# Norm of the query latent: its four tiles' squares are added on VectorE, and TensorE sums one tile instead of four

## The chip, the cores and the metric

The kernel runs on one core of one Trainium2 chip. The metric is the device time of one execution, in microseconds (us). Lower is better.

## The reference, cut to what matters

The program is two blocks one after the other: a gated convolution and attention block with its feed-forward part, then a block with an RWKV7 mixer and a latent attention mixer (MLA), each with residual and norms. The change lies at the start of the latent attention mixer:

```
def _rms_norm(x, g):
    xf = x.astype(jnp.float32)
    y = xf * lax.rsqrt(jnp.mean(xf * xf, axis=-1, keepdims=True) + RMS_EPS)
    return (y * g.astype(jnp.float32)).astype(x.dtype)

def _mla_mixer(x, pos, w_in, q_norm, w_q_up, kv_norm, w_kv_up, w_out):
    B, L, _ = x.shape
    H = MLA_HEADS                                   # 16
    h = x @ w_in
    c_q, c_kv, k_rope, g = jnp.split(h, [Q_LORA, Q_LORA + KV_LORA, Q_LORA + KV_LORA + QK_ROPE], axis=-1)
    q = (_rms_norm(c_q, q_norm) @ w_q_up).reshape(B, L, H, QK_NOPE + QK_ROPE)
    q_nope, q_rope = q[..., :QK_NOPE], _rope(q[..., QK_NOPE:], pos)
    kv = (_rms_norm(c_kv, kv_norm) @ w_kv_up).reshape(B, L, H, QK_NOPE + V_HEAD)
    k_nope, v = kv[..., :QK_NOPE], kv[..., QK_NOPE:]
    k_rope = _rope(k_rope, pos)
    o = _causal_block_attention(q_nope, q_rope, k_nope, k_rope, v).reshape(B, L, D_INNER)
    return (o * jax.nn.silu(g)) @ w_out
```

The query latent c_q has 512 features (4 tiles of 128), the key/value latent c_kv has 256 (2 tiles). There are 512 tokens, and 16 meta tokens ahead of them for the keys. The change is in how the mean of the squares of c_q is formed.

## The kernel before, in words

Features lie on the 128 partitions and tokens in the columns, so a norm's sum over features is a sum over partitions and tiles. ScalarE squares each tile into one of two slots of the buffer norm_sq (line 210). TensorE multiplies each slot with a 128 x 128 matrix of ones and accumulates all tiles in one PSUM bank (pe_tile, line 227). These operands are fp32, and the profile shows each such matmul as two. ScalarE then takes Ln (line 219) and Exp (line 221) for the reciprocal root.

Every matmul of the projections is three fp32r matmuls, high x high, low x high, high x low (product, lines 162 to 164). So each operand is split into a high and a low part. GpSimd splits the weights, unit by unit, with two instructions: w_hi (line 150) and w_lo (line 153). The split of unit u waits until TensorE has finished unit u - 2, whose buffer it takes. VectorE does the activations: for each latent tile a scaled product norm_y (line 245), a cast to the high part (line 250) and a subtraction for the low part (line 253).

The stretch around the change runs so. There are seven input units, 0 to 6, each of eight blocks of 128 features: units 0 to 3 make the query latent's tiles, 4 and 5 those of the key/value latent, 6 the rotary key. On TensorE come units 2, 3 and 4, the sums of norm_q, units 5 and 6, the sums of norm_kv, and then six "fills", products that prepare the first head: gate 0, rope, ka, qn, kb, gate 1 (lines 2822 to 2829 and the function fill at line 2312). Rope and qn need the query latent's four high and low parts, ka and kb those of the key/value latent. Kb also needs its bank back from the rope fill, which VectorE's first rope instruction (line 2424) reads. After the fills head 0 starts, and its first value product needs the weight unit "B 0", whose split on GpSimd waits for the end of VectorE's rope group (q_step, lines 2439 and 2441). GpSimd's splits are in the order: input units, gate 0, A 0 (weights of rope, ka, qn and kb), gate 1, B 0.

VectorE works through one fixed list (lines 2925 to 2972): the four tiles cq out of PSUM (line 2927), tile 0 of ckv (line 2933), cos_r and sin_r (lines 2937 and 2938), norm_q tiles 0 and 1, ckv tile 1 (line 2933), norm_q tiles 2 and 3, five small memsets (lines 2949 and 2950), the rotary key's product (line 2953), norm_kv tiles 0 and 1, the gate out of PSUM (line 2402), and the rope group (lines 2960 to 2968 and 2424 to 2441). ScalarE's list there is: the four squares of cq, Ln and Exp, the two squares of ckv, Ln and Exp, k_sw, the gate's Silu (line 2396), and the rope copies q_sw (line 2376, four instructions) that the rope instruction of line 2424 waits for. Since the Silu is ahead of q_sw and waits for line 2402, the rope group follows line 2402.

The counters: sq_ready counts squares done, sq_summed tiles summed. The square of tile j waits for sq_summed to show that its slot has been read.

Of the kernel before, what the change touches and what calls it, by code (L numbers as in the profile page):

```python
# [12 lines left out]
ALU = mybir.AluOpType  # L13
# [57 lines left out]
def program(nc, io, out):  # L71
    with ExitStack() as base:
        def sb(name, shape, dt=F32, stack=base):
            return stack.enter_context(nc.sbuf_tensor(name, shape, dt))
# [4 lines left out]
        def sem(name):  # L79
            return base.enter_context(nc.semaphore(name))  # L80
# [19 lines left out]
        ps = base.enter_context(nc.psum_tensor("ps", [P, 8, 512], F32))  # L100
# [3 lines left out]
        ones = sb("ones", [P, P])  # L104
# [21 lines left out]
        def prm(name, j=0, n=1):  # L126
            return params[:, COL[name] + j:COL[name] + j + n]
# [5 lines left out]
        def load_unit(sp, u, s, src, first=False):  # L133
            if not first:
                sp.wait_ge(split_ready, u - 1)
            _, k, n = src.shape
            sp.dma_start(raw[s][:, 0:k * n].rearrange("p (k n) -> p k n", k=k), src).then_inc(landed[s], 16)
# [36 lines left out]
        sq_ready = sem("sq_ready")  # L174
        sq_summed = sem("sq_summed")
# [10 lines left out]
        class Norm:  # L186
# [12 lines left out]
                tiles_before[0] += tiles  # L199
                norms_before[0] += 1  # L200

            def act(self, act, wait_x, last=None):
                for j in range(self.tiles):
                    wait_x(act, j)
                    if self.t0 + j >= 2:
                        act.wait_ge(sq_summed, self.t0 + j - 1)
                    dst, src = self.sq[:, j % 2, 0:self.cols], self.x(j)
                    if last is not None and j == self.tiles - 1:
                        dst, src = dst.rearrange("p (a b) -> p a b", a=2), last
                    nc.scalar.activation(dst, src, ACT.Square).then_inc(sq_ready, 1)  # L210
                self.act_r(act)
# [12 lines left out]
            def pe_tile(self, pe, j):  # L224
                pe.wait_ge(sq_ready, self.t0 + j + 1)
                for h, (at, n) in enumerate(self.halves):
                    mm = nc.tensor.matmul(ps[:, self.bank + h, 0:n], ones[:], self.sq[:, j % 2, at:at + n],  # L227
                                          start=(j == 0), stop=(j == self.tiles - 1))
                mm.then_inc(sq_summed, 1)

            def pe(self, pe):
# [39 lines left out]
            def act_parts(self, act, hi, p0):  # L271
                for j in range(self.tiles):
                    act.wait_ge(y_ready, self.t0 + j + 1)
                    nc.scalar.activation(hi(j), self.y[:, j % 4, 0:self.cols], ACT.Copy).then_inc(act_hi_ready, 1)
# [1881 lines left out]
        norm_q = Norm(lambda j: cq[:, j, :], 4, HALVES1, 512, lambda j: prm("qn", j), 6, put.end)  # L2156
# [15 lines left out]
        s_tab, in_ev, k_step = sem("s_tab"), sem("in_ev"), sem("k_step")  # L2172
# [525 lines left out]
        with nc.Block() as block:  # L2698
# [75 lines left out]
            def _(pe):  # L2774
# [11 lines left out]
                def in_unit(n, banks, parts):  # L2786
                    u = U_IN + n
                    pe.wait_ge(split_ready, u + 1)
                    for k in range(KD):
                        for b, (at, cols) in zip(banks, parts):  # L2790
                            mm = product(ps[:, b, 0:cols], block_of(slot_of(u), k), (u2_hi[:, k, at:at + cols], u2_lo[:, k, at:at + cols]),
                                         k == 0, k == KD - 1)
                    mm.then_inc(unit_done, 1)
# [10 lines left out]
                for i, j in enumerate(WO_ORDER):  # L2804
# [3 lines left out]
                    for t in range(QB):  # L2808
                        mm = nc.tensor.transpose(ps[:, 2 + i % 2, P * t:P * t + P], xT[:, j, N_META + P * t:N_META + P * t + P], ident[:])
# [9 lines left out]
                in_unit(2, (2,), TAIL)  # L2819
                in_unit(3, (3,), TAIL)  # L2820
                in_unit(4, (4, 5), HALVES2)
                norm_q.pe(pe)
                pe.wait_ge(in_ev, 2)
                in_unit(5, (0, 1), HALVES2)
                pe.wait_ge(in_ev, 4)
# [9 lines left out]
            def _(act):  # L2835
# [5 lines left out]
                               last=ps[:, WO_BANKS[WO_ORDER[-1]][0]:WO_BANKS[WO_ORDER[-1]][1] + 1, 0:T2 // 2])  # L2841

                def rows_out(i):
                    j = WO_ORDER[i]
                    act.wait_ge(x_turned, KD + i + 1)
                    nc.scalar.activation(h_rows[:, :, P * j:P * j + P], ps[:, 2 + i % 2, :].rearrange("p (a b) -> p a b", b=P),
                                         ACT.Copy).then_inc(x_copied, 1)
# [6 lines left out]
                        rows_out(i - 1)  # L2854
                norm_pre1.act_r(act)
                rows_out(KD - 1)
                norm_q.act(act, lambda e, j: e.wait_ge(in_ev, j + 1))
                norm_kv.act(act, lambda e, j: e.wait_ge(in_ev, j + 5))
                act.wait_ge(k_step, 3)
                for q in range(4):  # L2860
# [14 lines left out]
                for half in range(2):  # L2875
                    act.wait_ge(o_mm, QB + half)
                    at = (t, 2 * QB)[half]
# [10 lines left out]
            def _(dve):  # L2888
                front_dve(dve)
                all_passes(dve, pass_dve)  # L2890
                for j, m in enumerate(WO_ORDER):
                    dst = mT[:, m, :].rearrange("p (a b) -> p a b", a=2)
# [32 lines left out]
                for m in range(4):  # L2925
                    dve.wait_ge(unit_done, U_IN + m + 1)
                    nc.vector.tensor_tensor(cq[:, m, :], ps[:, m, :], r_pre1[:, N_META:T2], ALU.mult).then_inc(in_ev, 1)
                two = lambda ap: ap.rearrange("p (a b) -> p a b", a=2)

                def ckv_out(m):  # L2930
# [93 lines left out]
```

## Time and profile before

| what | value |
|---|---|
| time, median of 3 runs | 2260.21 us (2258.67 to 2261.58) |
| the profiled execution's own time | 2259.74 us |
| its span | 2258.0 us |
| granted TensorE clock in the span | 0.998 of full speed |
| busy: TensorE | 2226.6 us, 99% |
| busy: VectorE | 1212.6 us, 54% |
| busy: ScalarE | 838.4 us, 37% |
| busy: GpSimd | 1155.2 us, 51% |
| matmuls in the span | 21811 |

The span is the time from the first to the last instruction in the trace; the execution's own time is 1.74 us longer. PE is TensorE, DVE VectorE, ACT ScalarE, POOL GpSimd. A row of the timeline gives start and length of an instruction in us, then in brackets how long the engine had stood idle before it and what released it. A busy TensorE may still be waiting in part: the ends of its matmuls are modelled, so a stall shows best in its weight loads.

### The profile page before, as it was taken

Reading aid. Unit: us, or ns where it says so; the run is one execution under the profiler, and the core shown is the slowest. Engines: PE = TensorE matmul, PEld = TensorE weight load, DVE = VectorE, ACT = ScalarE, POOL = GpSimd, SP = SyncE. Lnnn points to the kernel's source line nnn. Section 1 sums busy time; section 2 is a strip of 40 time slices with the busy share of each in tenths; the row PEclk is TensorE's granted clock in tenths of the full one; section 3 lists DMA queues with packets and bytes.
Section 4 is the critical chain, followed back from the end, with each engine's and each line's share of the span. In section 5 each row is a group of like instructions: output and inputs, shape, how many; then the busy total and the mean of one; then the engine's idle time right before and its main releaser. Section 6 shows DMA issues by size and latency. Waiting matters only on the chain.

```text
span 2258.0 us, 51404 instructions
## 1 busy us (share of the span) xinstructions
PE 2226.6 (99%) x21811; PEld 1798.7 (80%) x21811; DVE 1212.6 (54%) x2314; ACT 838.4 (37%) x1725; POOL 1155.2 (51%) x802
## 2 busy tenths in 40 slices
PE   8999999999999999999999999999999999999998
PEld 7788888788888677777777777777889788888877
DVE  4353357877830955555555555666540475555521
ACT  4122212333310455555555555555421344434311
POOL 4555567687766163444444444444636353443454
PEclk9999999999999999999999999999999999999999
DMA  3323333333332122222222222222413322212132
GB/s 117 85 76 83 80 88 93 94 94 99 97 105 92 49 90 67 70 77 72 73 79 84 72 70 71 77 70 97 167 55 112 113 71 56 64 51 55 52 126 89
DMA packets 262108, 188.04 MB, mean 83 GB/s; under 512 B 18283, under 2 KB 242409, under 8 KB 261497
## 3 DMA queue, kind: packets, MB, share of 16 engines
q1 hardware_dynamic: 261881, 184.76, 27.3%
q8 instruction: 174, 2.85, 0.5%
q14 instruction: 53, 0.43, 0.1%
HBM read 162.69 MB, written 22.04 MB: 82 GB/s over the span
## 4 chain that ended last, share of the span: by engine, by line
PE 94%; DVE 3%; POOL 1%; ACT 1%; SPq 0%; issue 0%; DMA 0%; DVEq 0%; POOLq 0%; ACTq 0%
PE ps L1359 20%; PE ps L162 17%; PE ps L163 16%; PE ps L164 16%; PE ps L1545 3%; PE ps L1561 3%; PE ps L1587 2%; PE ps L2509 2%; PE ps L1534 2%; PE ps L1372 1%; PE ps L1501 1%; PE ps L227 1%; PE ps L1473 1%; PE ps L1490 1%; PE ps L1523 1%; PE ps L1459 1%
## 5 line engine op out<-in xcount | busy, mean ns | idle before, releaser
L153 POOL TENSOR_TENSOR w_lo<-raw,w_hi 128x1024 fp32r<-128x1024 f32 (+1 forms) x164 | 418.8, 2554 | 13.7
L150 POOL TENSOR_SCALAR w_hi<-raw 128x1024 fp32r<-128x1024 f32 (+1 forms) x164 | 181.6, 1107 | 450.5 <-PE ps L164 434.5
L162 PE MATMUL ps<-h_hi,w_hi 128*128 128x512 f32 x616 | 243.8, 396 | 1.8 <-DVE h_lo L1068 1.7
L164 PE MATMUL ps<-h_hi,w_lo 128*128 128x512 f32 x616 | 240.6, 391 | 0.0
L163 PE MATMUL ps<-h_lo,w_hi 128*128 128x512 f32 x616 | 240.3, 390 | 0.0
L1359 PE MATMUL ps<-mixed_k,raw 128*64 128x264 f32 x1024 | 149.3, 387 | 0.0
L1359 PE MATMUL ps<-mixed_r,raw 128*64 128x264 f32 x1024 | 143.9, 387 | 0.0
L1359 PE MATMUL ps<-mixed_g,raw 128*64 128x264 f32 x1024 | 138.0, 386 | 0.0
L162 PEld LDWEIGHTS ps<-h_hi,w_hi 128*128 128x128 f32 x616 | 116.2, 189 | 25.9 <-DVE h_lo L1068 2.5
L164 PEld LDWEIGHTS ps<-h_hi,w_lo 128*128 128x128 f32 x616 | 116.0, 188 | 24.9
L163 PEld LDWEIGHTS ps<-h_lo,w_hi 128*128 128x128 f32 x616 | 116.2, 189 | 23.1
L1359 PE MATMUL ps<-mixed_v,raw 128*64 128x264 f32 x1024 | 129.0, 389 | 0.0
L1083 DVE SCALAR_TENSOR_TENSOR up_c<-up_raw,params,up_c 128x512 f32<-128x512 f32 x88 | 114.5, 1304 | 22.7 <-ACT up_c L838 21.1
L1887 DVE TENSOR_TENSOR x_m<-ps,lv_pad 128x640 f32<-128x640 f32 (+2 forms) x160 | 110.9, 726 | 9.7 <-PE ps L1545 5.2
L1951 POOL TENSOR_TENSOR kp<-k_b,kp 128x528 f32<-128x528 f32 x16 | 29.6, 1850 | 168.8 <-ACT kp L1680 168.8
L1545 PEld LDWEIGHTS ps<-t_m,mb 128*64 128x64 f32 x2752 | 95.9, 138 | 15.6 <-ACT mb L1668 3.4
L1545 PE MATMUL ps<-t_m,mb 128*64 128x64 f32 x2752 | 97.3, 222 | 0.2 <-DVE t_m L1893 0.2
L1359 PEld LDWEIGHTS ps<-mixed_v,raw 128*64 128x64 f32 x1024 | 69.6, 137 | 34.2 <-issue 2.5
L1968 POOL MEMSET uv<- 64x64 f32 x32 | 4.6, 145 | 175.2 <-PE ps L1516 174.3
L2615 ACT ACTIVATE xT<-ps,nmax 128x144 f32<-128x144 f32 (+1 forms) x64 | 34.4, 539 | 147.3 <-DVE nmax L2642 146.9
L1634 ACT ACTIVATE uv<-ps 64x64 f32<-64x64 f32 x128 | 27.9, 218 | 161.6 <-PE ps L1490 161.6
L1561 PEld LDWEIGHTS ps<-x_m,t_t 128*64 128x64 f32 x2240 | 77.5, 138 | 9.6 <-DVE x_m L1887 0.6
(473 smaller groups left out, 5973.4 us busy)
## 6 DMA issues: line engine op xcount, KB each, us to landing
raw<-in_rwkv_w_in_dram SPq DMA_DIRECT2D x64, 512.0 KB, 4.2
raw<-in_w_up_dram SPq DMA_DIRECT2D x44, 512.0 KB, 3.8
raw<-in_w_in_dram SPq DMA_DIRECT2D x41, 512.0 KB, 3.9
raw<-in_w_down_dram SPq DMA_DIRECT2D x22, 512.0 KB, 3.6
raw<-in_mla_w_in_dram SPq DMA_DIRECT2D x22, 512.0 KB, 4.1
sb_kept<-xT SPq DMA_DIRECT2D x16, 528.0 KB, 2.7
xT<-sb_kept SPq DMA_DIRECT2D x16, 528.0 KB, 4.6
raw<-in_rwkv_w_out_dram SPq DMA_DIRECT2D x16, 512.0 KB, 3.9
```

Of the source, the lines that this page charges most:

```text
L150: nc.gpsimd.tensor_scalar(w_hi[s][:, 0:width], raw[s][:, 0:width], 1.0, 0.0, ALU.mult, ALU.add).then_inc(split_hi, 1)
L153: nc.gpsimd.tensor_tensor(w_lo[s][:, 0:width], raw[s][:, 0:width], w_hi[s][:, 0:width].bitcast(F32), ALU.subtract).then_inc(split_ready, 1)
L162: nc.tensor.matmul(dst, w[0], x[0], start=start, stop=False)
L163: nc.tensor.matmul(dst, w[0], x[1], start=False, stop=False)
L164: return nc.tensor.matmul(dst, w[1], x[0], start=False, stop=stop)
L1083: nc.vector.scalar_tensor_tensor(out=up_c[:, ab, 1 + k, :], in0=up_raw[:, n % 4, 1 - k:1 - k + T1], scalar=prm(("cf1", "cf0")[k], n // 2 + ...
L1359: mm = nc.tensor.matmul(dst[m, :], raw_k[t % 2][:, k, m], mixed[t][:, k, cols], start=(k == 0), stop=(k == KD - 1))
L1534: mm = nc.tensor.matmul(ps[:, 2 + 3 * h + q, x * P:x * P + P], bk[own[h], c0 + x, :], rkv[own[h], c0 + x, 0:2 * C], start=True, stop=True)
L1545: mm = nc.tensor.matmul(ps[own[h], 2 + p, x * C:x * C + C], mb[:, c0 + x, own[h]], t_m[:, c0 + x, :], start=True, stop=True)
L1561: mm = nc.tensor.matmul(dst, t_t[:, c0 + x, :], x_m[:, c0 + x, h, :], start=True, stop=True)
L1587: mm = nc.tensor.matmul(ps[m, 6 + h, 0:T2 // 2], halves_ones[:, m], src(h), start=True, stop=True)
L1887: nc.vector.tensor_tensor(x_m[:, c0:c0 + m, :, :], part_of(2 + p, m).unsqueeze(2).to_broadcast([P, m, 2, C]), lv_pad[:, lv - 1, :, :].unsq ...
```

## The change

In norm_q alone, ScalarE still squares four tiles, but tile 0 goes to slot 0 and tiles 1, 2 and 3 all go to slot 1. After each of tiles 1 to 3 VectorE adds slot 1 to slot 0. TensorE then multiplies slot 0 once with the ones. The adds and the one sum count up sq_summed as the four sums did.

```diff
-            def act(self, act, wait_x, last=None):
+            def act(self, act, wait_x, last=None, added=False):
                 for j in range(self.tiles):
                     wait_x(act, j)
                     if self.t0 + j >= 2:
                         act.wait_ge(sq_summed, self.t0 + j - 1)
-                    dst, src = self.sq[:, j % 2, 0:self.cols], self.x(j)
+                    dst, src = self.sq[:, min(j, 1) if added else j % 2, 0:self.cols], self.x(j)
...
+            def dve_add(self, dve, j):
+                dve.wait_ge(sq_ready, self.t0 + j + 1)
+                if j >= 2:
+                    dve.wait_ge(sq_summed, self.t0 + j - 1)
+                acc = self.sq[:, 0, 0:self.cols]
+                nc.vector.tensor_tensor(acc, acc, self.sq[:, 1, 0:self.cols], ALU.add).then_inc(sq_summed, 1)
+
+            def pe_slot(self, pe, slot, first, last):
+                for h, (at, n) in enumerate(self.halves):
+                    mm = nc.tensor.matmul(ps[:, self.bank + h, 0:n], ones[:], self.sq[:, slot, at:at + n], start=first, stop=last)
                 mm.then_inc(sq_summed, 1)
...
                 in_unit(4, (4, 5), HALVES2)
-                norm_q.pe(pe)
+                pe.wait_ge(sq_summed, norm_q.t0 + norm_q.tiles - 1)
+                norm_q.pe_slot(pe, 0, True, True)
                 pe.wait_ge(in_ev, 2)
...
-                norm_q.act(act, lambda e, j: e.wait_ge(in_ev, j + 1))
+                norm_q.act(act, lambda e, j: e.wait_ge(in_ev, j + 1), added=True)
...
                 for m in range(4):
                     dve.wait_ge(unit_done, U_IN + m + 1)
                     nc.vector.tensor_tensor(cq[:, m, :], ps[:, m, :], r_pre1[:, N_META:T2], ALU.mult).then_inc(in_ev, 1)
+                    if m:
+                        norm_q.dve_add(dve, m)
```

On VectorE, from the query latent's first tile on, the list before is (cq, ckv: the latents' tiles; ps: PSUM; r_pre: the factor of the norm ahead of the mixer):

```order
L2927 TENSOR_TENSOR cq<-ps,r_pre 128x512 [waits unit_done,rs_ready]
L2927 TENSOR_TENSOR cq<-ps,r_pre 128x512 [waits unit_done] x3
L2933 TENSOR_TENSOR ckv<-ps,r_pre 128x528 [waits unit_done]
L2937 TENSOR_TENSOR cos_r<-cos_t,r_pre 128x528 [waits s_tab,in_ev]
L2938 TENSOR_TENSOR sin_r<-sin_t,r_pre 128x528
L245 SCALAR_TENSOR_TENSOR norm_y<-cq,params,norm_r 128x512 [waits rs_ready]
```

and with the change:

```order
L2940 TENSOR_TENSOR cq<-ps,r_pre 128x512 [waits unit_done,rs_ready]
L2940 TENSOR_TENSOR cq<-ps,r_pre 128x512 [waits unit_done]
L236 TENSOR_TENSOR norm_sq<-norm_sq 128x512 [waits sq_ready]
L2940 TENSOR_TENSOR cq<-ps,r_pre 128x512 [waits unit_done]
L236 TENSOR_TENSOR norm_sq<-norm_sq 128x512 [waits sq_summed,sq_ready]
L2940 TENSOR_TENSOR cq<-ps,r_pre 128x512 [waits unit_done]
L236 TENSOR_TENSOR norm_sq<-norm_sq 128x512 [waits sq_summed,sq_ready]
L2948 TENSOR_TENSOR ckv<-ps,r_pre 128x528 [waits unit_done]
L2952 TENSOR_TENSOR cos_r<-cos_t,r_pre 128x528 [waits s_tab,in_ev]
L2953 TENSOR_TENSOR sin_r<-sin_t,r_pre 128x528
L257 SCALAR_TENSOR_TENSOR norm_y<-cq,params,norm_r 128x512 [waits rs_ready]
```

Each of the last three tiles of cq has an add behind it that waits for that tile's square. Everything from ckv on keeps its order; lines 245, 250, 253, 2927 and 2933 are lines 257, 262, 265, 2940 and 2948 of the changed kernel.

On TensorE, from the last product of input unit 4 to the first of unit 5, the list before is:

```order
L162 MATMUL ps<-u_hi,w_hi 128x264
L163 MATMUL ps<-u_lo,w_hi 128x264
L164 MATMUL ps<-u_hi,w_lo 128x264
L227 MATMUL ps<-norm_sq,ones 128x512 [waits sq_ready] x4
L162 MATMUL ps<-u_hi,w_hi 128x264 [waits split_ready,in_ev]
L163 MATMUL ps<-u_lo,w_hi 128x264
```

and with the change:

```order
L162 MATMUL ps<-u_hi,w_hi 128x264
L163 MATMUL ps<-u_lo,w_hi 128x264
L164 MATMUL ps<-u_hi,w_lo 128x264
L240 MATMUL ps<-norm_sq,ones 128x512 [waits sq_summed]
L162 MATMUL ps<-u_hi,w_hi 128x264 [waits split_ready,in_ev]
L163 MATMUL ps<-u_lo,w_hi 128x264
```

Three of four sums are gone, and the one left waits for the adds (sq_summed) in place of the squares (sq_ready).

## Rows read from the trace of the kernel before

**Rows 1.** First line of the page.

```profile
span 2258.0 us, 51404 instructions
```

**Rows 2.** Busy us (and instructions) by engine in one stretch, PEclk, DMA share, GB/s.

```profile
1860.00:2030.00 170.00, 170.00 (x1015) 144.78 (x1014) 90.42 (x240) 70.36 (x140) 72.58 (x41) 1.00 0.21 57
```

**Rows 3.** Chain that ended last, in order: start us, us, what.

```profile
1804.08 3.62 PE ps L227 x8
...
1837.01 1.27 POOL w_hi L150
...
1841.36 0.39 PE ps L162
```

**Rows 4.** Timeline of TensorE's weight loads: start, length, instruction, [idle before <-releaser].

```profile
1804.34 0.19 PEld L227 LDWEIGHTS ps<-norm_sq,ones 128*128 128x128 f32 x1 [0.24 <-issue]
1804.77 0.19 PEld L227 LDWEIGHTS ps<-norm_sq,ones 128*128 128x128 f32 x1 [0.24 <-issue]
...
1805.71 0.30 PEld L227 LDWEIGHTS ps<-norm_sq,ones 128*128 128x128 f32 x2 [0.75 <-ACT norm_sq L210]
```

**Rows 5.** Timeline of ScalarE around the norm of the query latent.

```profile
1805.03 0.63 ACT L210 ACTIVATE norm_sq<-cq 128x512 f32<-128x512 f32 x1 [16.78 <-PE ps L227]
```

**Rows 6.** Timeline of VectorE, from the latent's last tile to the first gate.

```profile
1798.31 0.69 DVE L2927 TENSOR_TENSOR cq<-ps,r_pre 128x512 f32<-128x512 f32 x1 [4.87 <-PE ps L164]
...
1805.91 2.87 DVE L2938 TENSOR_TENSOR sin_r<-sin_t,r_pre 128x528 f32<-128x528 f32 x1
...
1809.12 0.75 DVE L245 SCALAR_TENSOR_TENSOR norm_y<-cq,params,norm_r 128x512 f32<-128x512 f32 x1 [0.35 <-ACT norm_r L221]
...
1813.53 0.71 DVE L2933 TENSOR_TENSOR ckv<-ps,r_pre 128x528 f32<-128x528 f32 x1 [0.62 <-PE ps L164]
...
1815.40 2.51 DVE L250 CAST cq_hi<-norm_y 128x512 fp32r<-128x512 f32 x1
...
1819.80 1.62 DVE L253 TENSOR_TENSOR cq_lo<-norm_y,cq_hi 128x512 fp32r<-128x512 f32 x1
...
1822.59 2.20 DVE L245 SCALAR_TENSOR_TENSOR norm_y<-ckv,params,norm_r 128x528 f32<-128x528 f32 x1 [0.25 <-ACT norm_r L221]
...
1827.19 1.43 DVE L253 TENSOR_TENSOR ckv_lo<-norm_y,ckv_hi 128x528 fp32r<-128x528 f32 x1
...
1828.54 0.68 DVE L2402 TENSOR_TENSOR gate<-ps,r_pre 128x512 f32<-128x512 f32 x1
```

**Rows 7.** Timeline of GpSimd: the splits of the weight units in this stretch.

```profile
1799.69 2.40 POOL L153 TENSOR_TENSOR w_lo<-raw,w_hi 128x1024 fp32r<-128x1024 f32 x1
...
1805.51 2.70 POOL L153 TENSOR_TENSOR w_lo<-raw,w_hi 128x1024 fp32r<-128x1024 f32 x1
...
1813.78 1.05 POOL L150 TENSOR_SCALAR w_hi<-raw 128x1024 fp32r<-128x1024 f32 x1 [5.57 <-PE ps L164]
...
1814.92 2.71 POOL L153 TENSOR_TENSOR w_lo<-raw,w_hi 128x1024 fp32r<-128x1024 f32 x1
...
1819.61 1.27 POOL L150 TENSOR_SCALAR w_hi<-raw 128x1280 fp32r<-128x1280 f32 x1 [1.98 <-PE ps L164]
...
1820.96 3.27 POOL L153 TENSOR_TENSOR w_lo<-raw,w_hi 128x1280 fp32r<-128x1280 f32 x1
...
1826.92 1.14 POOL L150 TENSOR_SCALAR w_hi<-raw 128x1024 fp32r<-128x1024 f32 x1 [2.69 <-PE ps L164]
```

**Rows 8.** Instructions of four VectorE lines: ns min/median/max, first and last start us, forms.

```profile
L245 DVE SCALAR_TENSOR_TENSOR norm_y<-cq,params,norm_r x4: 746/750/1211, 1809.1 to 1818.6; 128x512 f32<-128x512 f32 x4
...
L250 DVE CAST cq_hi<-norm_y x4: 426/428/2506, 1809.9 to 1819.3; 128x512 fp32r<-128x512 f32 x4
...
L253 DVE TENSOR_TENSOR cq_lo<-norm_y,cq_hi x4: 693/693/1619, 1810.4 to 1819.8; 128x512 fp32r<-128x512 f32 x4
...
L1059 DVE TENSOR_TENSOR ffn_sq<-ffn_sq x6: 687/1232/1376, 351.1 to 378.3; 128x512 f32<-128x512 f32 x6
```

**Rows 9.** Timeline of TensorE: first matmul of the fill ka.

```profile
1829.21 0.28 PE L162 MATMUL ps<-ckv_hi,w_hi 128*128 128x264 f32 x1
```

More of the change, by code:

```diff
@@ L228, in pe_tile @@
                                           start=(j == 0), stop=(j == self.tiles - 1))
+                mm.then_inc(sq_summed, 1)
+            def dve_add(self, dve, j):
[7 more added lines that the diff above has]
+                    mm = nc.tensor.matmul(ps[:, self.bank + h, 0:n], ones[:], self.sq[:, slot, at:at + n], start=first, stop=last)
                 mm.then_inc(sq_summed, 1)
```

## The prediction

> **What bounds the kernel now.** I read the page first, then the chain of waits and the timelines of all four engines from 1798 to 1842 us, where the changed instructions lie. The span is 2258.0 us [rows 1], and the execution that was profiled took 2259.74 us. TensorE is the bound nearly everywhere: between 1860 and 2030 us it was busy for the whole 170.00 us at full clock, with VectorE at 90.42 and GpSimd at 72.58 us [rows 2]. A microsecond that TensorE gains or loses before 1860 us therefore reaches the end. But the chain doesn't stay on TensorE in the stretch itself. From the sums of the key/value norm it runs over ScalarE and VectorE to GpSimd's split of unit B 0 at 1837.01 us and comes back to TensorE only at 1841.36 us [rows 3]. So two clocks run side by side from 1804 to 1841 us, TensorE's and VectorE's, and the later one decides.
>
> **What the change removes on TensorE.** The four sums take 3.62 us of the chain [rows 3]. Each is two passes of 512 columns. The weight loads of successive passes start at 1804.34 and 1804.77, so a pass costs 0.43 us and a sum 0.86 us; 4 x 0.86 = 3.44 us, and the rest is a wait for squares that ScalarE could only make once sum 0 had freed its slot: it stood idle for 16.78 us before the third square [rows 5], and the weight load for it began at 1805.71 after 0.75 us of idleness [rows 4]. One sum of 0.86 us is left, so TensorE starts unit 5 about 3.62 - 0.86 = 2.76 us earlier. Bounds: 3 x 0.86 = 2.58 us if the wait was hidden in part, 2.9 us at most.
>
> **What it adds on VectorE.** Three adds of two SBUF tiles, 128 x 512 fp32. The same operation stands elsewhere in this program at line 1059, with 0.687 us at least and 1.376 us at most [rows 8]; alone it is 0.69 us. Only the last could delay the sum. Tile 3 of cq starts at 1798.31 and takes 0.69 us [rows 6], its square 0.63 us [rows 5], so the add can start at 1799.7 us, just when GpSimd begins a w_lo of 2.40 us [rows 7]. If it has to wait for that, it ends near 1802.7 us; TensorE asks at 1803.9 us (0.17 us before the chain's 1804.08), and ckv tile 0, the next item of VectorE's list, is not released before 1804.1. If the add goes first, GpSimd ends its split near 1802.7 us in place of 1802.09, and TensorE needs it at 1804.8 us. The adds cost nothing at either end; the covers are 1.2 and 2.1 us. For the earlier adds VectorE has some 5 us of idle time each, as in the 4.87 us ahead of 1798.31. ScalarE no longer waits for sum 0, and Ln and Exp of norm_q end at about 1806.3 us.
>
> **What is late next.** The question is what VectorE makes of the 2.76 us. sin_r keeps it busy to 1808.78 us in any case (1805.91 + 2.87), which is only 0.35 us before it took up norm_q tile 0 in the trace [rows 6]. The other idle times on its path to the last low part of ckv are 0.62 us ahead of ckv tile 1 and 0.25 us ahead of norm_kv: 1.22 us in all. So VectorE can't gain more than 1.2 us, while TensorE comes 2.8 us earlier.
>
> It can lose, though, by GpSimd. Rows 8 give the three steps of a tile at 0.75, 0.43 and 0.69 us when undisturbed, but 1.21, 2.51 and 1.62 us at most. Each long one stands beside a split: the cast that started at 1815.40 ended at 1817.91, 0.28 us after GpSimd's w_lo (1814.92 + 2.71 = 1817.63); the low part from 1819.80 waited for the w_hi of 1819.61, norm_y from 1822.59 for the w_lo of 1820.96, the low part from 1827.19 for the w_hi of 1826.92, and sin_r for the w_lo of 1805.51 [rows 6, 7]. Instructions that read PSUM (ckv at 1813.53, the gate at 1828.54) were not lengthened. GpSimd is held back as well: its w_lo take 2.70, 2.71 and 3.27 us where one without VectorE beside it takes 2.40. So one of the two runs at a time. A waiting VectorE instruction ends 0.15 us less than its length after GpSimd's end, and GpSimd's waiting instruction 0.14 us less than its length after VectorE's end: 2.26 us for w_lo (1817.63 against 1815.37, just ahead of the cast), 2.81 us for the wide one of A 0 (1824.23 against 1821.42).
>
> In the trace these stalls on VectorE's path are 0.46 + 2.08 (gate 0), 0.93 + 1.44 (A 0) and 0.72 us (gate 1) = 5.6 us. The splits are released by TensorE, so they all come 2.76 us earlier, at 1811.02, 1816.85 and 1824.16 us, and VectorE's list comes only 0.35 us earlier. I walk through it with these lengths (ends of instructions, us):
> - norm_y 0 starts at 1808.72; norm_y 1 ends at 1811.33. w_hi of gate 0 was waiting, ends 1812.24; cast 1 1812.52; w_lo 1814.78; low part 1 1815.32; ckv tile 1 1815.96; its square 1816.6, still in time for TensorE's second sum of norm_kv at about 1817.2.
> - norm_y 2 1816.64; cast 2 1817.11; w_hi of A 0 1818.24; low part 2 1818.78; w_lo 1821.59; norm_y 3 1822.19; cast 3 1822.66; low part 3 1823.38. The memsets and the key product take 0.9 us as before (1821.42 to 1822.59 less 0.25 of idleness).
> - norm_kv: norm_y 0 would start at 1824.25, w_hi of gate 1 is ahead of it at 1824.16 and ends 1825.21; norm_y 0 1825.82; w_lo 1828.08; cast 0 1828.37; low part 0 1829.12; norm_y 1 1829.80; cast 1 1830.27; low part 1 1831.01.
>
> The stalls are now 0.7 + 2.1, 0.95 + 2.7 and 0.8 + 2.1 = 9.4 us, 3.7 more, against 1.2 us less idle time. What was hidden under TensorE's sums was that the splits fell beside waits and PSUM reads: the w_lo of gate 1 met the gate's PSUM read at 1828.54 and now meets the cast. Before, the low part ended at 1828.62 (1827.19 + 1.43), 0.6 us before TensorE began ka at 1829.21 [rows 9]. Now TensorE asks at 1829.21 - 2.76 = 1826.45 us and waits some 4.6 us. The end is 1831.01 - 1828.62 = 2.4 us later than before.
>
> That is handed on. Behind the low part come the gate (1830.9), the Silu, four q_sw and the rope group, which releases B 0's split and also kb's bank. Each followed the one before it directly in the trace, so the split of 1837.01 and TensorE's return at 1841.36 [rows 3] come 2.4 us later, and TensorE's own work between ka and there, some 12 us, starts 1.9 us late and gets its other 0.5 us as a wait for kb's bank. **Sum: 2.4 us slower.** Against the profiled execution 2259.74 + 2.4 = 2262.1 us; the median of the three runs stands 0.47 us above that execution, which gives 2260.21 + 2.4 = 2262.6 us. I take the second.
>
> **A rule of the Trainium skill beside this.** The row is sin_r: 2.87 us at 1805.91, against 0.69 us for a subtraction of two SBUF tiles by itself [rows 6, 8]. The Trainium skill, page "SBUF — State Buffer", section "Who interferes with whom", says that a VectorE instruction with two SBUF inputs, or in a two-port mode, and a GpSimd instruction that reads SBUF lock each other out, that the earlier one has the shared pair for its whole length, and that a VectorE instruction with at most one SBUF input and outside those modes goes free. By that rule the trace agrees, and the rule decides an order that I can't know: if norm_y 0 of norm_kv takes the lock ahead of w_hi at 1824.2 us, the same walk ends at 1830.9 us in place of 1831.0. If the two shared in proportion and nobody waited for a whole instruction, the stalls would stay near 5.6 us and the first rival below would hold.
>
> **The rivals.**
> - A, the stalls stay as they are (5.6 us), because the order in which waiting instructions get through isn't the one of my walk. VectorE's path then ends 1.2 us earlier, at 1827.4 us, later than TensorE's 1826.45, so VectorE sets the time: 2260.2 - 1.2 = 2259.0 us. For it: I have only five stalls to read the order from. Against: all five fit.
> - B, TensorE's gain goes through whole: 2260.2 - 2.8 = 2257.4 us. For it: TensorE is the 99% engine. Against: VectorE would have to reach the last low part of ckv by 1826.4 us, 2.2 us before its old end, with only 1.2 us of idle time to give; a split would have to miss it altogether.
> - C, slower by over 0.2%: a further w_lo falls on VectorE's path, in the rope group or in head 0. Its place would be B 0's or gate 2's split against the instructions that TensorE's first attention products wait for. Its price is one more stall of up to 2.7 us, the largest of the walk, so 2.4 + 2.7 = 5.1 us and 2265.3 us. It decides if the shift isn't the same on GpSimd and VectorE after 1837 us. Against: B 0's split is released by VectorE's own group, so both shift together.
>
> **How the numbers follow.** The forecast has a chance of 0.64, A 0.14, B 0.10, C 0.12. What a measurement of this kernel can tell from no change is about 0.2%, 4.5 us. The forecast lies inside it unless the spread of the runs (2258.67 to 2261.58) adds 2 us (0.04), A and B lie inside, C lies just over it (0.07 of its 0.12). So: slower 0.11, faster 0.03, within 0.2% 0.86. The range runs from 2257.8 us (A and part of B's spread) to 2265.2 us (most of C). The forecast by itself spans 2261.1 to 2264.1 us, the same width as the three runs.
>
> **What would show each step.** Right: one sum with two passes ends near 1804.8 us; the adds end before 1803.9; unit 5 starts 2.8 us earlier; a cast or low part beside each w_lo is 2.5 to 2.8 us long; norm_y 3 is near 3.5 us; the last low part of ckv ends near 1831 us; TensorE's weight loads show a gap of 4 to 5 us ahead of ka; B 0's split starts near 1839.4 us. Wrong: ka follows rope with no gap (B), or a gap near 1 us and B 0's split at 1835.8 (A), or an add or a late split ahead of the sum or of unit 5, which would upset the 2.76 us itself.

## The result, and the profile after

The changed kernel takes 2263.21 us (median of 20 runs, 2260.99 to 2266.79) against 2260.45 us (20 runs, 2258.63 to 2261.93) for the kernel before. The ratio is 1.0014 with a 95% interval of 1.0008 to 1.002: it is slower, by 2.8 us, less than the 0.2% that the forecast called no change. The forecast was 2262.6 us, with a range of 2257.8 to 2265.2 us.

The page of the changed kernel, first line and the line of busy times (engine, us, share of the span, instructions):

```profile
span 2260.9 us, 51397 instructions
...
PE 2225.9 (98%) x21805; PEld 1801.3 (80%) x21805; DVE 1223.5 (54%) x2317; ACT 840.9 (37%) x1725; POOL 1157.2 (51%) x802
```

VectorE has three instructions more and TensorE six fewer, as the change says; the span is 2.9 us longer [rows 1]. Of these 2.9 us, 0.69 us were there before the stretch in question: ckv tile 0 starts at 1804.80 us against 1804.11. Executions of one kernel differ by as much and more ahead of 1800 us (e5 and e12 below are one kernel and start this tile at 1802.51 and 1804.37 us), so from here on times are taken from the start of ckv tile 0, in what I call the **interval**: from there to head 0's first value product (w_hi, ckv_hi) on TensorE. Before it is 1841.36 - 1804.11 = 37.25 us.

VectorE's timeline of the changed kernel, with the lines that answer to [rows 6]:

```profile
1799.01 0.69 DVE L2940 TENSOR_TENSOR cq<-ps,r_pre 128x512 f32<-128x512 f32 x1 [3.48 <-PE ps L164]
1800.40 2.93 DVE L236 TENSOR_TENSOR norm_sq<-norm_sq 128x512 f32<-128x512 f32 x1 [0.70 <-ACT norm_sq L210]
1804.80 0.71 DVE L2948 TENSOR_TENSOR ckv<-ps,r_pre 128x528 f32<-128x528 f32 x1 [1.47 <-PE ps L164]
...
1806.60 2.90 DVE L2953 TENSOR_TENSOR sin_r<-sin_t,r_pre 128x528 f32<-128x528 f32 x1
1809.42 0.74 DVE L257 SCALAR_TENSOR_TENSOR norm_y<-cq,params,norm_r 128x512 f32<-128x512 f32 x1
...
1812.05 1.15 DVE L262 CAST cq_hi<-norm_y 128x512 fp32r<-128x512 f32 x1
1813.24 2.77 DVE L265 TENSOR_TENSOR cq_lo<-norm_y,cq_hi 128x512 fp32r<-128x512 f32 x1
1815.93 0.69 DVE L2948 TENSOR_TENSOR ckv<-ps,r_pre 128x528 f32<-128x528 f32 x1
...
1817.78 1.62 DVE L265 TENSOR_TENSOR cq_lo<-norm_y,cq_hi 128x512 fp32r<-128x512 f32 x1
1819.32 3.45 DVE L257 SCALAR_TENSOR_TENSOR norm_y<-cq,params,norm_r 128x512 f32<-128x512 f32 x1
...
1824.80 0.76 DVE L257 SCALAR_TENSOR_TENSOR norm_y<-ckv,params,norm_r 128x528 f32<-128x528 f32 x1
1825.60 1.16 DVE L262 CAST ckv_hi<-norm_y 128x528 fp32r<-128x528 f32 x1
1826.79 2.73 DVE L265 TENSOR_TENSOR ckv_lo<-norm_y,ckv_hi 128x528 fp32r<-128x528 f32 x1
...
1830.71 0.71 DVE L265 TENSOR_TENSOR ckv_lo<-norm_y,ckv_hi 128x528 fp32r<-128x528 f32 x1
1831.34 0.69 DVE L2414 TENSOR_TENSOR gate<-ps,r_pre 128x512 f32<-128x512 f32 x1
```

And GpSimd's, which answer to [rows 7]:

```profile
1800.39 2.40 POOL L153 TENSOR_TENSOR w_lo<-raw,w_hi 128x1024 fp32r<-128x1024 f32 x1
...
1811.72 1.20 POOL L150 TENSOR_SCALAR w_hi<-raw 128x1024 fp32r<-128x1024 f32 x1 [2.79 <-PE ps L164]
1813.01 2.45 POOL L153 TENSOR_TENSOR w_lo<-raw,w_hi 128x1024 fp32r<-128x1024 f32 x1
1817.55 1.32 POOL L150 TENSOR_SCALAR w_hi<-raw 128x1280 fp32r<-128x1280 f32 x1 [2.09 <-PE ps L164]
1818.94 3.28 POOL L153 TENSOR_TENSOR w_lo<-raw,w_hi 128x1280 fp32r<-128x1280 f32 x1
1824.86 1.61 POOL L150 TENSOR_SCALAR w_hi<-raw 128x1024 fp32r<-128x1024 f32 x1 [2.64 <-PE ps L164]
1826.56 2.41 POOL L153 TENSOR_TENSOR w_lo<-raw,w_hi 128x1024 fp32r<-128x1024 f32 x1
1839.81 1.26 POOL L150 TENSOR_SCALAR w_hi<-raw 128x1280 fp32r<-128x1280 f32 x1 [10.85 <-DVE qr L2453]
```

The last add waited for the w_lo of 1800.39 and took 2.93 us, and was done 1.5 us before ckv tile 0. sin_r kept its 2.90 us. Then come the stalls: cast 1 took 1.15 us and low part 1 2.77 us beside gate 0's split (1811.72 and 1813.01), low part 2 1.62 us and norm_y 3 3.45 us beside A 0's (1817.55 and 1818.94), and in norm_kv cast 0 1.16 us and low part 0 2.73 us beside gate 1's (1824.86 and 1826.56). Each ends 0.3 to 0.6 us after a GpSimd instruction does. The last low part of ckv ends at 1831.42 us, 26.62 us after ckv tile 0 began; before it was 24.51 us.

TensorE's weight loads, and the first value product on TensorE (these answer to [rows 3, 4, 9]):

```profile
1804.49 0.31 PEld L240 LDWEIGHTS ps<-norm_sq,ones 128*128 128x128 f32 x2
1805.04 0.19 PEld L162 LDWEIGHTS ps<-u_hi,w_hi 128*128 128x128 f32 x1 [0.24 <-issue]
...
1831.54 0.19 PEld L162 LDWEIGHTS ps<-ckv_hi,w_hi 128*128 128x128 f32 x1 [4.65 <-issue]
```

```profile
1844.30 0.36 PE L162 MATMUL ps<-w_hi,ckv_hi 128*128 128x256 f32 x1
```

The one sum's two loads are at 1804.49 and unit 5's first at 1805.04. Ahead of ka TensorE stood for 4.65 us by its loads (4.26 by the matmuls' own idle time) and began it at 1831.57 us, which is 1.67 us later in the interval than in [rows 9]. The interval is 1844.30 - 1804.80 = 39.50 us, 2.25 us longer than before; with the 0.69 us from ahead of it this makes the 2.9 us of the span.

One thing the forecast had not: the clock. The stretches in and behind the gap (us, busy us of PE, PEld, DVE, ACT, POOL with counts, granted clock, DMA share, GB/s):

```profile
1827.00:1831.50 4.50, 0.31 (x2) 0.00 (x0) 4.43 (x5) 1.66 (x2) 1.96 (x1) 1.00 0.27 67
1831.50:1833.50 2.00, 1.93 (x8) 1.79 (x9) 1.85 (x3) 1.41 (x3) 0.00 (x0) 0.62 0.37 111
1833.50:1835.50 2.00, 2.00 (x6) 1.62 (x5) 0.36 (x1) 1.95 (x4) 0.00 (x0) 0.52 0.00 0
1835.50:1837.50 2.00, 2.00 (x13) 1.75 (x13) 1.97 (x5) 0.63 (x2) 0.00 (x0) 1.00 0.00 0
```

After 4.3 us of idleness the granted clock was 0.62 and then 0.52 in two windows of 2 us. Full speed is 2.4 GHz and the lower level 1.2 GHz, 0.5 of it, so TensorE stood at the lower level for 0.76 + 0.96 of a window, 3.4 of these 4.0 us. In the kernel before it was 1.00 throughout this stretch.

### The profile page after: what moved, and what is told of

Read it like the earlier page. It is cut to its first block, busy times and chain, and to the rows that moved or that the text cites. A ratio compares the mean times of both kernels' runs of the same rounds, so it can differ in the third digit from the quotient of the medians.

```text
span 2260.9 us, 51397 instructions
## 1 busy us (share of the span) xinstructions
PE 2225.9 (98%) x21805; PEld 1801.3 (80%) x21805; DVE 1223.5 (54%) x2317; ACT 840.9 (37%) x1725; POOL 1157.2 (51%) x802
## 4 chain that ended last, share of the span: by engine, by line
PE 94%; DVE 3%; POOL 1%; ACT 1%; SPq 0%; issue 0%; DMA 0%; DVEq 0%; POOLq 0%; ACTq 0%
PE ps L1371 20%; PE ps L162 17%; PE ps L163 16%; PE ps L164 16%; PE ps L1557 3%; PE ps L1573 3%; PE ps L1599 2%; PE ps L2521 2%; PE ps L1546 2%; PE ps L1384 1%; PE ps L1513 1%; PE ps L1485 1%; PE ps L1502 1%; PE ps L1535 1%; PE ps L1471 1%; PE ps L2504 1%
## 5 line engine op out<-in xcount | busy, mean ns | idle before, releaser
L162 PEld LDWEIGHTS ps<-h_hi,w_hi 128*128 128x128 f32 x616 | 115.8, 188 | 26.2 <-DVE h_lo L1080 2.8
L1095 DVE SCALAR_TENSOR_TENSOR up_c<-up_raw,params,up_c 128x512 f32<-128x512 f32 x88 | 119.1, 1357 | 20.3 <-ACT up_c L850 18.7
```

The lines of the kernel that those rows point to most:

```text
L162: nc.tensor.matmul(dst, w[0], x[0], start=start, stop=False)
L1095: nc.vector.scalar_tensor_tensor(out=up_c[:, ab, 1 + k, :], in0=up_raw[:, n % 4, 1 - k:1 - k + T1], scalar=prm(("cf1", "cf0")[k], n // 2 + ...
```

## The experiments

Each kernel was timed 11 times beside the kernel before on the same chip. A time comparison of that size has a 95% interval of about 0.09% (2 us) to either side, so the medians decide little and the intervals inside the profiled executions decide most. There is one profiled execution of each kernel. The interval of one kernel repeated where that could be seen: the kernel that was run twice under two names (e5 and e12) showed 35.88 us both times. From the first value product to the end every execution took the same 416.6 to 416.7 us, so two spans differ by the start of ckv tile 0 and by the interval.

| kernel | interval, us | last low part of ckv, us after ckv tile 0 | ratio of times to before (95%) |
|---|---|---|---|
| before | 37.25 | 24.51 | |
| changed | 39.50 | 26.62 | 1.0014 (1.0008 to 1.002) |
| e1, no adds | 39.52 | 26.62 | 1.0012 (1.0003 to 1.002) |
| e2, three sums more | 37.07 | 24.33 | 0.9993 (0.9984 to 1.0002) |
| e8, one sum more | 38.98 | 26.08 | 1.0009 (1.0 to 1.0018) |
| e3, gate 1's split held | 37.39 | 23.86 | 0.9997 (0.9988 to 1.0006) |
| e4, gap filled | 39.35 | 26.62 | 1.0011 (1.0002 to 1.002) |
| e7, tables early | 37.91 | 25.17 | 0.9999 (0.999 to 1.0008) |
| e5 and again e12, early and held | 35.88, 35.88 | 22.34, 22.35 | 0.9996 (0.9987 to 1.0004), 0.9995 (0.9986 to 1.0004) |
| e6, early and held, on before | 37.33 | 23.78 | 1.0004 (0.9995 to 1.0013) |
| e9, q_sw first | 40.61 | 26.61 | 1.001 (1.0001 to 1.0019) |
| e10, q_sw first and gap filled | 37.93 | 26.62 | 1.0004 (0.9996 to 1.0013) |
| e11, rope first | 35.87 | 22.35 | 1.0 (0.9991 to 1.0009) |

**e1: are the adds to blame?** In dve_add the sum is left out; waits and counts stay.

```diff
-                nc.vector.tensor_tensor(acc, acc, self.sq[:, 1, 0:self.cols], ALU.add).then_inc(sq_summed, 1)
+                dve.sem_inc(sq_summed, 1)
```

> The changed kernel with the three adds left out (VectorE keeps their waits and counts up the semaphore), so that the norm of the query latent is taken over tile 0 alone. TensorE's and GpSimd's timing is that of the changed kernel. Theory L (GpSimd's splits and VectorE's list lock each other out once the splits come 2.8 us earlier; the adds cost nothing): the loss stays, 2.8 us over before as in the changed kernel (within 0.7 us), the last low part of ckv about 26.6 us after ckv tile 0 starts, a gap of 4 to 5 us ahead of ka. Rival R1 (the three adds on VectorE cost the time): back to before or below, at or under +0.5 us.

The interval is 39.52 us and the last low part comes after 26.62 us, both as with the adds, to 0.02 us. The time is 3.55 us over before by medians, at the edge of what was allowed. The three adds cost nothing; R1 falls.

**e2: TensorE's timing put back.**

```diff
+                for _ in range(3):
+                    nc.tensor.matmul(ps[:, 6, 0:512], ones[:], norm_q.sq[:, 0, 0:512], start=True, stop=True)
                 norm_q.pe_slot(pe, 0, True, True)
```

> The changed kernel with three sums of the same slot put ahead of the one sum on TensorE, so that TensorE reaches unit 5 nearly when it did before (4 x 0.86 = 3.44 us of sums against 3.62 us), while the adds stay. Theory L: the time is that of before, between -0.5 and +0.7 us, the last low part of ckv about 24.5 us after ckv tile 0 starts, no gap ahead of ka, no low clock there. R1 (the adds cost it): still +2.8 us.

VectorE's timeline of this kernel:

```profile
1802.67 0.71 DVE L2950 TENSOR_TENSOR ckv<-ps,r_pre 128x528 f32<-128x528 f32 x1 [1.47 <-PE ps L164]
...
1813.78 2.51 DVE L262 CAST cq_hi<-norm_y 128x512 fp32r<-128x512 f32 x1
...
1825.57 1.43 DVE L265 TENSOR_TENSOR ckv_lo<-norm_y,ckv_hi 128x528 fp32r<-128x528 f32 x1
```

The cast is 2.51 us and the last low part 1.43 us, the very durations of [rows 6]. The interval is 37.07 us, 0.18 us under before, which is what 3.44 us of sums in place of 3.62 give. The time's median is 1.5 us under before, outside the half microsecond that was allowed, with an interval that holds no difference; I take it for the spread of the runs. With the adds in place and only TensorE's work put back, the loss is gone: it comes from TensorE's earlier start.

**e8: half the shift.** The same edit with one sum more in place of three.

> The changed kernel with one more sum on TensorE (two in place of one; TensorE reaches unit 5 1.9 us earlier than before, in place of 2.76). Theory L gives by the walk: the last low part of ckv 26.2 us after ckv tile 0 starts (before 24.5, changed 26.6), interval to the first value product 38.9 us, time 1.7 us over before. A loss in proportion to TensorE's gain would be 1.9/2.76 of 2.25 us, 1.55 us; a loss by the clock after the gap alone would be smaller than that.

The interval is 38.98 us (38.9 expected) and the last low part 26.08 us (26.2). The walk through the locks holds for a shift it wasn't made from. In proportion it would have been 38.8 us, so the interval alone can't tell the walk from that. The single lengths can: the longest instructions were the cast of cq tile 2 (2.51 us), the low part of cq tile 3 (3.33 us) and the cast of ckv tile 1 (2.47 us), other ones than in the changed kernel. The median is 3.5 us over before where 1.7 were expected; the ratio's interval (0 to 4 us) holds both.

**e3: one split taken out of VectorE's way.**

```diff
             def split_mla(pool, u):
+                if u == UNIT_AT["gate", 1]:
+                    pool.wait_ge(y_lo_ready, CKV_READY)
```

> The changed kernel with one wait more on GpSimd: the split of weight unit gate 1 waits for the last low part of ckv. Theory L: the stalls of that split (0.8 + 2.1 us in the walk) leave VectorE's path; the last low part ends about 2.8 us earlier than in the changed kernel, the gap ahead of ka shrinks from 4.3 us to 1.5 to 2 us, and the time is 2.5 to 3.5 us under the changed kernel, which is before -0.4 us within 0.7. Rival R2 (the place where VectorE and GpSimd meet doesn't matter, TensorE is late for another reason, as the lower clock after the gap): no more than 1 us under the changed kernel.

Its VectorE timeline, from ckv tile 0 on:

```profile
1806.72 0.71 DVE L2950 TENSOR_TENSOR ckv<-ps,r_pre 128x528 f32<-128x528 f32 x1 [1.47 <-PE ps L164]
...
1827.51 0.43 DVE L262 CAST ckv_hi<-norm_y 128x528 fp32r<-128x528 f32 x1
1827.97 0.71 DVE L265 TENSOR_TENSOR ckv_lo<-norm_y,ckv_hi 128x528 fp32r<-128x528 f32 x1
...
1829.87 0.71 DVE L265 TENSOR_TENSOR ckv_lo<-norm_y,ckv_hi 128x528 fp32r<-128x528 f32 x1
```

Cast 0 and low part 0 of ckv are back at 0.43 and 0.71 us, from 1.16 and 2.73. The last low part ends 2.76 us earlier in the interval than in the changed kernel, the gap ahead of ka is 1.5 us, and the interval is 2.11 us shorter, 0.14 us over before. The time is 0.25 us under before by medians, as expected; the interval gave up less than the last low part did, since the held split now meets the rotary key's product (1.27 us in place of 0.70) and its sum (2.79 us in place of 0.71), and q_rot kept kb waiting for 1.6 us. So without this one pair of stalls 2.1 of the 2.25 us are gone. That TensorE's clock stayed at 1.00 behind the shorter gap is part of this edit too; e4 separates the two and leaves the clock, which R2 names, 0.15 us; R2 falls.

**e4: the gap filled with sums, for the clock.**

```diff
                 for n in range(6):
+                    if n == 2:
+                        for _ in range(5):
+                            nc.tensor.matmul(ps[:, 1, 0:512], ones[:], norm_q.sq[:, 0, 0:512], start=True, stop=True)
                     fill(pe, n)
```

> The changed kernel with five more sums (ten passes, 4.3 us) into a spare PSUM bank ahead of ka on TensorE, which fill the gap where TensorE waits for VectorE. In the changed kernel the granted clock was 0.62 and 0.52 of full in the 4 us behind that gap. Theory C (beside L: the idle gap lowers the clock; in the profiled execution B 0's split hides it, in others it lasts longer and costs up to 4 us, which is the upper group of the 20 runs at 2264.6 to 2266.8): clock 1.00 behind ka, median 0.5 to 1.5 us under the changed kernel, no run over 2264.5. If the clock costs nothing: the same median and the same spread. If the sums themselves delay ka: 0.3 us over it.

The clock stayed at 1.00 and the interval is 39.35 us, 0.15 us under the changed kernel. The median is 0.7 us under the changed kernel's, which was not timed beside it. Theory C is wrong in its second half: the upper group of times stayed (up to 2266.17 us in 11 runs), and in this profiled execution ckv tile 0 started only at 1808.40 us. Such differences are made ahead of the stretch, and the traces show where most of them come from: the granted clock falls there in some executions and not in others, though all kernels do the same work up to 1780 us. The windows from 1650 to 1700 us of e4, and then of e3:

```profile
1650.00:1700.00 50.00, 48.29 (x592) 40.25 (x590) 17.35 (x51) 9.95 (x26) 18.29 (x12) 0.93 0.19 54
```

```profile
1650.00:1700.00 50.00, 48.28 (x612) 40.42 (x612) 17.89 (x52) 11.77 (x29) 18.32 (x12) 1.00 0.22 65
```

A VectorE copy at 1662.46 us in e4 stands at 1662.30 in e3; its third follower stands at 1675.34 against 1672.39 us, so the low clock cost 2.8 us there. A clock of 0.97 between 1600 and 1700 us have e1, e4, e10 and e11, one of 0.98 between 0 and 100 us the changed kernel, e1, e3, e4, e9 and e11. Those with both reached ckv tile 0 at 1808.40 to 1808.49 us, those with one at 1804.80 to 1807.05, and those with neither at 1802.51 to 1804.37 us; before, at 1804.11, had its 0.98 between 400 and 500 us. The single times go with it: of the changed kernel's 20 runs the five of 2266.26 to 2266.79 us have a clock of 0.994 or 0.995 over the whole execution, the four of 2260.99 to 2261.33 us have 0.997. Why the clock falls at these places in one execution and not in another stays open.

**e7, e5, e6: an earlier start of VectorE's list.** cos_r and sin_r are made in VectorE's idle time between the tiles of cq.

```diff
                 for m in range(4):
...
+                    if m == 1:
+                        dve.wait_ge(s_tab, 64)
+                        nc.vector.tensor_tensor(cos_r[:], cos_t[:], r_pre1[:], ALU.mult).then_inc(k_step, 1)
+                    if m == 2:
+                        nc.vector.tensor_tensor(sin_r[:], sin_t[:], r_pre1[:], ALU.mult).then_inc(k_step, 1)
...
                 ckv_out(0)
-                dve.wait_ge(in_ev, 5)
-                dve.wait_ge(s_tab, 64)
-                nc.vector.tensor_tensor(cos_r[:], cos_t[:], r_pre1[:], ALU.mult).then_inc(k_step, 1)
-                nc.vector.tensor_tensor(sin_r[:], sin_t[:], r_pre1[:], ALU.mult).then_inc(k_step, 1)
```

e7 has this edit on the changed kernel, e5 has it with e3's, and e6 has both edits on the kernel before.

> The changed kernel with cos_r and sin_r early and gate 1's split where it was. Theory L: the last low part of ckv ends 25.3 us after ckv tile 0 starts, the interval to the first value product is 38.0 us, time 0.8 us over before (0 to 1.6). If only the start of VectorE's list counted and not the locks: 2.4 us under the changed kernel, at 37.1 us.

> The changed kernel with cos_r made behind tile 1 and sin_r behind tile 2 of cq, in VectorE's idle time there, and with gate 1's split held until the last low part of ckv. Theory L, by the same walk of locks: norm_y 0 waits for ScalarE and the w_lo of unit 6 and ends 4.4 us after ckv tile 0 starts, and the last low part of ckv ends 22.4 us after it, 2.1 us earlier than in before, so TensorE's gain comes through but for 0.6 us. From ckv tile 0 to head 0's first value product: 35.2 us (before 37.25, changed 39.50). Time 2.1 us under before (1.4 to 2.8). Rival R3 (the early cos_r and sin_r collide with splits 3 and 4 and delay unit 5 or the squares, so that the gain is lost): no better than the kernel with gate 1's split held alone.

> The kernel before with the same two edits (early cos_r and sin_r, gate 1's split held) and without the change to the norm. Theory L: norm_y 0 waits here for the reciprocal root and not for sin_r, so the early tables give nothing, and the held split takes 0.7 us off VectorE's path, of which TensorE can use 0.6 (0.45 us wait ahead of kb, 0.18 ahead of the first value product). Interval from ckv tile 0 to the first value product 36.6 us, time 0.6 us under before. If instead the gain of the kernel with both came from these edits alone, it would be 2.1 us under before here too.

For e7 the walk gave 25.3 and 38.0 us; measured 25.17 and 37.91. For e5 it gave 22.4 and 35.2; measured 22.34 and 35.88. VectorE and the first value product in e5:

```profile
1802.51 0.71 DVE L2955 TENSOR_TENSOR ckv<-ps,r_pre 128x528 f32<-128x528 f32 x1 [1.47 <-PE ps L164]
1804.75 2.11 DVE L257 SCALAR_TENSOR_TENSOR norm_y<-cq,params,norm_r 128x512 f32<-128x512 f32 x1 [1.54 <-ACT norm_r L221]
...
1824.14 0.71 DVE L265 TENSOR_TENSOR ckv_lo<-norm_y,ckv_hi 128x528 fp32r<-128x528 f32 x1
...
1826.67 2.79 DVE L2980 TENSOR_TENSOR cos_r<-cos_r,k_sw 128x528 f32<-128x528 f32 x1
```

```profile
1838.39 0.39 PE L162 MATMUL ps<-w_hi,ckv_hi 128*128 128x256 f32 x1 [0.19 <-POOL w_lo L153]
```

The last low part is where it should be. What I had missed is behind it: the sum of the rotary key (cos_r, 1826.67) stood for 2.79 us behind gate 1's held w_lo, and the rope group behind that. The same happened in e6 (2.79 us too), whose interval of 37.33 us is not the 36.6 us expected, though its last low part came 0.7 us earlier. So the two edits alone bring nothing on the kernel before, and together with the change they end 1.37 us under before.

**e9 and e10: what the lower clock costs.** Both have ScalarE's q_sw ahead of the gate's Silu on the changed kernel, which frees B 0's split from the gate; e10 has e4's sums too.

```diff
+                fill_out(act, FILLS[1])
                 gate_silu(act, 0)
-                for n in range(1, 5):
+                for n in range(2, 5):
                     fill_out(act, FILLS[n])
```

> The changed kernel with ScalarE's four q_sw ahead of the gate's Silu, so that the rope group no longer waits for the gate behind the last low part: VectorE's rope instruction ends 2 us earlier and B 0's split no longer decides. What is left is TensorE itself: the gap ahead of ka and the lower clock behind it. Interval from ckv tile 0 to the first value product, by TensorE alone: theory T (the gap of 4.3 us and 3.7 us at half clock together make TensorE just as late as B 0's split): 39.3 to 39.5 us, no gain over the changed kernel's 39.50. If the low clock costs nothing and only B 0's split counted: 38.3 us.

> The kernel with q_sw first, and five more sums (4.3 us) in TensorE's gap ahead of ka, which keep its clock at 1.00. Theory T: both causes of the lateness are gone but the gap: interval 38.3 us (ka 1.7 us later than in before, less the 0.6 us that before waited for kb's bank and B 0), 1.0 to 1.2 us under the kernel without the sums, and that difference is what the low clock costs. If the clock costs nothing: no difference between the two kernels.

Windows of e9, and then of e10, behind the gap (columns as above; the clock is the third value from the end):

```profile
1832.00:1834.00 2.00, 0.20 (x1) 0.23 (x2) 1.93 (x4) 1.30 (x2) 0.00 (x0) 0.71 0.75 195
1834.00:1836.00 2.00, 2.00 (x8) 1.90 (x9) 1.97 (x4) 1.02 (x2) 0.00 (x0) 0.50 0.22 67
1836.00:1838.00 2.00, 2.00 (x6) 1.51 (x6) 1.97 (x5) 0.00 (x0) 0.00 (x0) 0.50 0.00 0
1838.00:1840.00 2.00, 2.00 (x7) 1.56 (x6) 1.93 (x4) 0.00 (x0) 0.00 (x0) 0.59 0.00 0
1840.00:1842.00 2.00, 2.00 (x13) 1.74 (x13) 1.05 (x3) 1.60 (x3) 0.74 (x1) 1.00 0.00 0
```

```profile
1832.00:1834.00 2.00, 2.00 (x11) 1.39 (x10) 1.97 (x4) 0.99 (x3) 0.00 (x0) 1.00 0.66 197
...
1838.00:1840.00 2.00, 2.00 (x10) 1.64 (x9) 1.77 (x4) 0.73 (x1) 1.04 (x1) 1.00 0.00 0
```

Two kernels that differ in the filling alone: 40.61 and 37.93 us, 2.68 us apart. In e9 the clock was at the lower level for 6.8 us in all (1.2 + 2.0 + 2.0 + 1.6 us by the windows), longer than the 3.4 us of the changed kernel's execution, and cost more than the 1.0 to 1.2 us expected; the interval was to be 39.3 to 39.5 us. Why the stretch at the lower level was longer is open. These are one execution of each kernel, and e9's own time, 2266.00 us, was its second longest of 11; by the medians the two kernels are 1.3 us apart, so 2.68 us may be more than the filling is usually worth. In e9 TensorE is the last: the first value product waited for nothing, and B 0's split was itself released by TensorE. e10 came to 37.93 us where 38.3 was expected.

**e11: rope ahead of the rotary key.** e5 with q_sw first and VectorE's rope instructions ahead of the rotary key's two.

> The kernel with the tables early and gate 1's split held, and beside it q_sw ahead of the gate's Silu on ScalarE and the rope instructions ahead of the rotary key's two on VectorE, so that the w_lo of gate 1 falls into VectorE's wait for q_sw. In the kernel without this the rotary key's sum stood 2.79 us behind that w_lo, and B 0's split started 31.5 us after ckv tile 0. Theory L: the wait ahead of kb (1.6 us) goes, B 0's split starts at about 31.2 us, interval to the first value product 35.5 us (35.88 without this), time 1.7 us under before. If another instruction takes the lost lock in its place: 35.9 us or more.

The 2.79 us stall is gone and kb no longer waits, but B 0's split starts 31.57 us after ckv tile 0, hardly later than e5's 31.54, since the rotary key's instructions now stand between the rope instructions and the last part of the rope group. The interval is 35.87 us, so the edit brings nothing; what had been a wait of 1.6 us ahead of kb is one of 1.76 us ahead of the first value product. Its times (2259.31 to 2263.01 us) don't show e5's gain. In its profiled execution (2262.78 us) that was lost ahead of the stretch: it had the low clock both between 0 and 100 and between 1600 and 1700 us and reached ckv tile 0 at 1808.49 us, 6.0 us later than e5's.

**e12: e5 once more.**

> The kernel with the tables early and gate 1's split held, once more, for a second measurement of its time: 1.4 us under before by its interval (35.88 against 37.25 us), within 0.9 us by the spread of such a comparison.

The interval is 35.88 us again. Pooled, 22 runs of e5 and e12 have a mean 1.35 us under that of 54 runs of before, with 0.8 us to either side at 95% (worked out from the single times), and a median of 2259.07 against 2260.46 us. By the interval it is the fastest version of this study, level with e11. The times don't rank it: the median of e2, whose interval is 1.2 us longer, was as low (2259.08 us). Its median lies some 4 us under the changed kernel's 2263.21, which was not timed beside it.

## Why the prediction was right

- **TensorE's gain.** 2.76 us were forecast from sums of 0.86 us. Unit 5's first weight load stands 0.24 us after ckv tile 0's start (1805.04 less 1804.80); in the kernel before it stood 3.00 us after it (1807.11 less 1804.11). The difference is 2.76 us.
- **The adds.** Forecast at nothing at either end. They took 0.69 us free and 2.93 us behind a w_lo, over the 1.376 us at most of [rows 8], and e1 shows that leaving them out changes the interval by 0.02 us. The last one took the worse end: it lost to the w_lo, ended at 1803.33 us, and TensorE's sum began at 1804.5.
- **The stalls.** Forecast 0.7 + 2.1, 0.95 + 2.7 and 0.8 + 2.1 us; measured, as length less the free length, 0.72 + 2.08, 0.93 + 2.70 and 0.73 + 2.02 us. At the third split VectorE took the lock first, not GpSimd as the walk had it, and the forecast's remark that the other order ends at 1830.9 in place of 1831.0 covers it: in the interval the last low part ended 0.3 us earlier than forecast, at 1830.73 us of the old time. 0.1 us of it was there by norm_y 3; about as much is the other order by that remark.
- **How it was handed on.** The forecast sent the whole 2.4 us through the gate, the Silu, q_sw and the rope group. B 0's split started 35.01 us after ckv tile 0 against 32.90 us, 2.11 us later, and TensorE came back 2.25 us later. That is the one step with a flaw: the forecast had TensorE waiting for kb's bank, but TensorE was late by itself, because the lower clock stretched ka and qn. It needed 12.73 us from ka to the first value product, and 11.16 us in e10, at full clock and without waits. The forecast's "some 12 us" of own work (12.15 us in the kernel before) had 0.45 us of waiting for kb's bank and 0.18 us for B 0 in it. TensorE and the split were equally late within 0.2 us. That the clock, which the forecast left out, didn't show in the sum is luck; e4 (0.15 us) shows how little it added on top, and e9 against e10 (2.68 us, one execution of each) shows that it costs more once nothing hides it.
- **The rivals.** A (stalls as before) and B (gain goes through) are refuted by the stall lengths; C's further stall didn't occur in the changed kernel, but such a stall, by gate 1's held w_lo in the rotary key's sum, is just what spoiled part of e3, e5 and e6.
- **The size.** 2.4 us forecast, 2.25 us in the interval, 2.8 us by the medians of 20 runs (1.8 to 4.5 us by the ratio's interval).

Of the expectations written after the result, e4's was wrong on the upper group, e5's, e6's and e11's on the rotary key's instructions, and e9's on how long the clock stays low. The medians of e2 and e8 lie further off than their intervals.

## What to carry to other kernels

TensorE at 99% doesn't mean that TensorE work taken away is time gained: find the next place where it waits for another engine and work out whether that engine can come earlier too. Where VectorE and GpSimd work on SBUF at once, walk their instructions through one lock in order of time, since a shift of one engine moves the collisions and not only the idle times. Then move the split or the VectorE work that collides: here holding one split took 2.1 us off the loss and making the tables early 1.6 us, and the two together, which did nothing for the kernel before, turned a loss of 2.25 us into a gain of 1.37 us. Compare such kernels by intervals inside an execution, and look at the clock of each stretch ahead of them before a difference of a few microseconds in the times is put down to an edit.

## What the runs showed of the hardware

- The lock between VectorE and GpSimd runs to hundredths: a cast of 2.51 us and a low part of 1.62 us came back in e2 as in before. A waiting instruction ends a little less than its own length after the other engine's end: 0.15 us less for the casts and low parts, 0.20 us for norm_y (3.45 us from 1819.32, behind the w_lo that ended at 1822.22), 0.14 to 0.19 us for GpSimd's instructions. In the collisions read here the two alternated when both had work waiting.
- An instruction that is held back may be short: a cast of 0.43 us took 2.51, and the longest, norm_y, 3.45 us in place of 0.75.
- After 4.3 us of idleness TensorE's clock was at the lower level for 3.4 us in the changed kernel and in e1, and for 6.8 us in e9, part of it still in the gap; after 2.9 us in e8 it averaged 0.79 over 8 us; after 2.8 us in e7 and 1.5 us in e3 it stayed at 1.00. It also fell where TensorE had not stood idle: in the changed kernel it was busy for 23.94 us of the 24 us from 26 to 50 us, at 1.00, and had a clock of 0.57 in the next 4 us.
- The times of one kernel spread over 2 to 6 us in 11 or 20 runs, and much of it is made well ahead of the change, by falls of the clock that one execution has and another hasn't: 2.8 us at 1662 us in e4. Intervals between two instructions inside one execution told differences of 0.2 us that the times could not.
